# Early modulation of a float32 two-block kernel: nine weight tiles as TensorE's stationary operand, seven on VectorE

## The reference, cut to what matters

```python
def adaln(cond, w, b):
    m = jax.nn.silu(cond) @ w + b
    return jnp.split(m, 3, axis=-1)           # shift, scale, gate

h  = rms_norm(x,   norm_g[0]) * (1 + scale)   + shift      # c     -> shift, scale
hc = rms_norm(ctx, norm_g[0]) * (1 + scale_c) + shift_c    # c_ctx -> shift_c, scale_c
p, pc = h @ w_in, hc @ w_in[:, COL_K:]        # attention and state-space mixer follow
```

## Time and profile before

| | us |
|---|---|
| median of 3 runs (2713.63 to 2717.82) | 2715.2 |
| the profiled execution's own time | 2714.01 |
| its span | 2711.8 |
| TensorE busy, of the span | 2670.9 (98%) |
| VectorE busy | 1667.5 (61%) |
| ScalarE busy | 467.1 (17%) |
| start of the first projection on TensorE, from the span's start | 133.39 |

### The profile page before, as it was taken

The page is one execution under the profiler, slowest core; times in us unless marked ns, Lnnn a source line. Parts: engine busy times, 40 slices in busy tenths (PEclk is TensorE's granted clock), DMA queues, the critical chain, the costliest instruction groups (busy, mean ns, idle before and its releaser), DMA issues. The chain is left out here.

```text
span 2711.8 us, 45920 instructions
## 1 busy us (share of the span) xinstructions
PE 2670.9 (98%) x19376; PEld 2409.5 (89%) x19376; DVE 1667.5 (61%) x2875; ACT 467.1 (17%) x918; POOL 51.3 (2%) x72
## 2 busy tenths in 40 slices
PE   6999999999999999999999999999999999999999
PEld 1399999999997877777778999999999999999999
DVE  3686767776675566666655536556566655555643
ACT  0231211121111222222220002111111111121211
POOL 0000000000000000000000000000000000000000
PEclk9999999999999999999999999999999999999999
DMA  9855755575545333333354455555554554455542
GB/s 387 306 166 198 228 179 182 187 243 169 187 152 183 115 113 113 112 112 112 112 201 154 149 164 171 171 163 177 156 180 159 155 156 146 144 150 158 162 136 82
DMA packets 381819, 453.86 MB, mean 167 GB/s; under 512 B 20596, under 2 KB 351848, under 8 KB 380648
## 3 DMA queue, kind: packets, MB, share of 16 engines
q1 hardware_dynamic: 351520, 356.69, 42.8%
q0 software_dynamic: 19520, 75.50, 7.7%
q10 hardware_dynamic: 10632, 19.51, 1.9%
HBM read 443.49 MB, written 8.19 MB: 167 GB/s over the span
## 5 line engine op out<-in xcount | busy, mean ns | idle before, releaser
L583 PE MATMUL bank<-hT,w 128*128 128x128 f32 (+2 forms) x6240 | 898.1, 302 | 6.1 <-ACT hT L1295 4.6
L583 PEld LDWEIGHTS bank<-hT,w 128*128 128x128 f32 x6240 | 786.7, 193 | 100.0 <-issue 85.4
L583 PE MATMUL bank<-yT,w 128*128 128x128 f32 (+1 forms) x3776 | 526.3, 299 | 1.0 <-DVE yT L2228 1.0
L583 PEld LDWEIGHTS bank<-yT,w 128*128 128x128 f32 x3776 | 493.2, 192 | 22.8 <-DVE yT L2228 1.2
L1295 ACT ACTIVATE work<-bank 128x512 f32<-128x512 f32 (+3 forms) x294 | 151.5, 522 | 1264.1 <-PE bank L583 1212.1
L583 PE MATMUL bank<-hT,work 128*128 128x128 f32 x2672 | 316.8, 275 | 0.0
L583 PEld LDWEIGHTS bank<-hT,work 128*128 128x128 f32 x2672 | 307.5, 192 | 0.0
L583 PEld LDWEIGHTS bank<-w,hT 128*128 128x128 f32 x1792 | 245.0, 191 | 19.3 <-issue 5.7
L583 PE MATMUL bank<-w,hT 128*128 128x128 f32 (+2 forms) x1792 | 261.4, 305 | 0.0
L1295 ACT ACTIVATE work<-work 128x512 f32<-128x512 f32 (+3 forms) x299 | 168.3, 569 | 276.1 <-DVE work L2078 156.3
L1923 DVE SCALAR_TENSOR_TENSOR work<-xT,silc,work 128x512 f32<-128x512 f32 x240 | 180.3, 751 | 33.5 <-DMA xT<-in_ada_w 26.7
(11 more groups left out here) (219 smaller groups left out, 2432.4 us busy)
## 6 DMA issues: line engine op xcount, KB each, us to landing
w<-in_na_ssd_w_in SPq DMA_DIRECT2D x48, 2048.0 KB, 11.4
xT<-in_ada_w POOLq DMA_DIRECT2D x64, 1024.0 KB, 8.6
w<-in_sc_w_in SPq DMA_DIRECT2D x32, 2048.0 KB, 10.2
w<-in_w_in SPq DMA_DIRECT2D x32, 2048.0 KB, 9.9
w<-in_na_ssd_w_out SPq DMA_DIRECT2D x16, 2048.0 KB, 9.5
w<-in_ada_w SPq DMA_DIRECT2D x12, 2048.0 KB, 12.0
w<-in_na_ssd_w_in SPq DMA_DIRECT2D x16, 1024.0 KB, 8.7
w<-in_sc_w_out SPq DMA_DIRECT2D x8, 2048.0 KB, 8.3
```

The lines of the kernel that those rows point to most:

```text
L583: return nc.tensor.matmul(dst, lhsT, rhs, start=start, stop=stop, skip_group_check=free)
```

## The change

Only the early part is written anew.

- TensorE takes nine tiles: (b 2, q 3) and all of blocks 0 and 1. The 128x128 pieces of the tile are now the **stationary** operand and the two columns of `sil` move: 32 matmuls a tile, each of two moving columns, that accumulate over the chunks and quarters straight into columns of bank 0 (shift) and bank 3 (scale). The rows in PSUM, VectorE's copies of them and `early_turn` go.
- VectorE takes seven tiles: all of block 3 and q 0 to 2 of block 2, through three places (`w[3]`, the low half of `yT`, and half of `hT` in 1 KB pieces), loaded by POOL's queue. Two `early_sums` of 16 matmuls each add its two accumulators to bank 3.
- The scale is finished first; VectorE does ten of the sixteen chunks of `first_norm(0)` before it takes the shift, which TensorE's last tile completes.
- `x` and `ctx` are turned apart, 32 transposes behind tile 0 and 32 behind tile 1; ScalarE alone copies them out, a bank (128x512) at a time. ScalarE squares the rows of the tokens with a running sum, and four small VectorE operations put the sums on diagonals (`diagonals`), in place of the reduction over 8192 elements a partition.
- `c` and `c_ctx` are loaded first, as 32 rows of their own; the other parameters come later. The last tile and the first projection's weights are loaded in halves. `x_columns` is stored after three loads of projection weights.

Core of the diff (blank lines left out):

```diff
-    arow = L(2, 4 * TILE)
-    eacc = L(2, 4 * TILE)
+    eaccs = {2: L(2, 4 * TILE), 3: L(2, 4 * TILE)}
+    crow, squares_of_rows, one_zero = L(P), L(4), L(4)
...
-    EARLY = 4
+    EARLY_PE = [(2, 3)] + [(b, q) for b in range(2) for q in range(4)]
+    EARLY_DVE = [(3, q) for q in range(4)] + [(2, q) for q in range(3)]
+    EARLY_SLOT = [0, 1, 2, 0, 1, 2, 1, 2, 3]
+    EARLY_PLACE = [0, 1, 2, 0, 1, 2, 1]
+    EARLY = [EARLY_SLOT.count(s) for s in range(SLOTS)]
...
+    early_places = [w3.rearrange("p (a b) -> p a b", a=4),
+                    yT[:, 0:DC, :].rearrange("p a b -> p (a b)").rearrange("p (a b) -> p a b", a=4),
+                    hT[:, :, 0:T]]
...
-        for t in range(4):
-            wait(gp, early_taken, t)
-            gp.dma_start(w3.rearrange("p (a b) -> p a b", a=4), w_ada[0][:, 4 * t:4 * t + 4, 12 * TILE:16 * TILE]).then_inc(
-                early_in, 16)
+        for t, (b, q) in enumerate(EARLY_DVE):
+            place = EARLY_PLACE[t]
+            earlier = [m for m in range(t) if EARLY_PLACE[m] == place]
+            if earlier:
+                gp.wait_ge(early_taken, earlier[-1] + 1)
+            if place < 2:
+                gp.dma_start(early_places[place], early_columns(b, q)).then_inc(early_v[place], 16)
+            else:
+                for kc in range(4):
+                    gp.dma_start(hT[:, 4 * kc:4 * kc + 4, 0:T], early_columns(b, q, (kc,)).rearrange(
+                        "p a (b c) -> p (a b) c", c=T)).then_inc(early_v[place], 16)
...
-        sp.dma_start(cst[:, :], ins["consts"]).then_inc(consts_in, 16)
+        sp.dma_start(IDENT, ins["consts"][:, 0:P]).then_inc(c_in, 16)
+        for k, src in enumerate((ins["c"][0], ins["c_ctx"])):
+            sp.dma_start(crow[16 * k:16 * k + 16, :], src.rearrange("(a b) -> a b", b=P)).then_inc(c_in, 16)
...
-        for u in range(12):
-            wait(sp, ada_used, u - 2)
-            sp.dma_start(early(u % 3), w_ada[0][:, 4 * (u % 4):4 * (u % 4) + 4, (u // 4) * 4 * TILE:(u // 4 + 1) * 4 * TILE]
-                         ).then_inc(w_loaded[u % 3], 16)
-        sp.wait_ge(xt_dve, DC // 2)
-        sp.wait_ge(xt_act, DC // 2)
-        sp.dma_start(x_scratch, xT[:, :, :].rearrange("p a b -> p (a b)")).then_inc(x_saved, 16)
+        for t, (b, q) in enumerate(EARLY_PE[:8]):
+            earlier = [m for m in range(t) if EARLY_SLOT[m] == EARLY_SLOT[t]]
+            if earlier:
+                sp.wait_ge(ada_used, earlier[-1] + 1)
+            sp.dma_start(early(EARLY_SLOT[t]), early_columns(b, q)).then_inc(w_loaded[EARLY_SLOT[t]], 16)
+        sp.wait_ge(early_taken, 4)
+        b, q = EARLY_PE[8]
+        sp.dma_start(early(3)[:, 0:2, :], early_columns(b, q, (0, 1))).then_inc(early_half, 16)
+        sp.dma_start(early(3)[:, 2:4, :], early_columns(b, q, (2, 3))).then_inc(w_loaded[3], 16)
...
+                sp.wait_ge(ada_used, (4, 7, 8)[n])
...
+        def rows_turned(k):
+            pe.wait_ge((x_in, ctx_in)[k], 32)
+            for m in range(EIGHT):
+                n = EIGHT * k + m
+                wait(pe, xt_act, n - 1)
+                for c in range(2):
+                    for tb in range(2):
+                        last = tr(bank[(1, 5)[n % 2]][:, (2 * c + tb) * P:(2 * c + tb + 1) * P],
+                                  xrow[:, 2 * k + tb, (2 * m + c) * P:(2 * m + c + 1) * P])
+                last.then_inc(xt_pe, 1)
...
+        def early_place(b, ch):
+            at = (b % 2) * 16 + ch * 2
+            return bank[0 if b < 2 else 3][:, at:at + 2]
+        def early_tile(t):
+            b, q = EARLY_PE[t]
+            s = EARLY_SLOT[t]
+            if t < 8:
+                pe.wait_ge(w_loaded[s], 16 * (1 + EARLY_SLOT[:t].count(s)))
+            else:
+                pe.wait_ge(early_half, 16)
             tile = w[s][:, :, :].rearrange("p a b -> p (a b)").rearrange("p (a b) -> p a b", a=4)
             for kc in range(4):
-                for half in range(2):
-                    last = mm(rows_of[half][0:2, :], pair[:, 4 * q + kc, :],
-                              tile[:, kc, half * 512:(half + 1) * 512], q + kc == 0, q + kc == 6)
+                if t == 8 and kc == 2:
+                    pe.wait_ge(w_loaded[3], 16)
+                for ch in range(8):
+                    last = mm(early_place(b, ch), tile[:, kc, ch * P:(ch + 1) * P], pair[:, 4 * q + kc, :],
+                              t < 2 and kc + ch == 0, t == 8 and kc + ch == 10, True)
             last.then_inc(ada_used, 1)
-            if u == 5:
-                pe.wait_ge(x_in, 64)
-                for kc in range(DC):
-                    x_turned(kc)
-            if u == 6:
-                early_turn(0)
-                pe.wait_ge(params_in, 16 * 17)
-                for n in range(1, 4):
-                    last = tr(bank[2][:, n * P:(n + 1) * P], prm[:, n, :])
-                last.then_inc(cols_pe, 1)
-            if u == 10:
-                early_turn(1)
+        def early_sums(b):
+            for ch in range(8):
+                for k in range(2):
+                    last = mm(early_place(b, ch), eaccs[b][:, k, ch * P:(ch + 1) * P], one_zero[:, 2 * k:2 * k + 2],
+                              False, b == 2 and ch + k == 8, True)
+            return last
+        early_tile(0)
+        rows_turned(0)
+        early_tile(1)
+        rows_turned(1)
+        early_tile(2)
+        pe.wait_ge(params_in, 16 * 19)
+        for n in range(4):
+            last = tr(bank[2][:, n * P:(n + 1) * P], prm[:, n, :])
+        last.then_inc(cols_pe, 1)
+        early_tile(3)
+        early_tile(4)
+        pe.wait_ge(consts_in, 16)
         pe.wait_ge(cols_dve, 2)
         norm_sums(0, T + TC)
+        early_tile(5)
         pe.wait_ge(early_taken, 4)
-        for ch in range(8):
-            for k in range(2):
-                n = 64 + 4 * ch + 2 * k
-                last = mm(bank[0][:, n:n + 2], eacc[:, k, ch * P:(ch + 1) * P], ONES[:, 0:2])
-        last.then_inc(ada_turned, 1)
-        early_turn(2)
+        early_sums(3)
+        early_tile(6)
+        early_tile(7)
+        pe.wait_ge(early_taken, 7)
+        early_sums(2).then_inc(ada_used, 1)
+        early_tile(8)
...
+            for k, columns in enumerate((xT, cxT)):
+                for m in range(EIGHT):
+                    n = EIGHT * k + m
+                    act.wait_ge(xt_pe, n + 1)
+                    A(columns[:, 2 * m:2 * m + 2, :], bank[(1, 5)[n % 2]][:, :].rearrange("p (a b) -> p a b", a=2),
+                      ACT.Copy).then_inc(xt_act, 1)
+                wait(act, norm_sq, k)
+                for tb in range(2):
+                    last = A(hT[:, EIGHT * tb:EIGHT * (tb + 1), T:2 * T],
+                             xrow[:, 2 * k + tb, :].rearrange("p (a b) -> p a b", a=EIGHT), ACT.Square,
+                             accum_out=squares_of_rows[:, 2 * k + tb:2 * k + tb + 1])
+                last.then_inc(norm_sq, 1)
...
+        def diagonals():
+            dve.wait_ge(c_in, 48)
+            dve.wait_ge(norm_sq, 2)
+            for tb in range(4):
+                last = v.tensor_scalar(ssq[:, tb * P:(tb + 1) * P], IDENT, squares_of_rows[:, tb:tb + 1], None, ALU.mult)
+            last.then_inc(norm_sum, 1)
...
+        for t in range(3):
+            early_part(t)
         dve.wait_ge(cols_pe, 2)
-        v.tensor_copy(colp[:, P:4 * P], bank[2][:, P:4 * P]).then_inc(cols_dve, 1)
-        early_part(2)
-        early_rows(1)
-        norm_sum_squares(0, 2, T + TC)
-        early_part(3)
-        early_rows(2)
+        v.tensor_copy(colp[:, :], bank[2][:, :]).then_inc(cols_dve, 1)
+        diagonals()
+        for t in range(3, 7):
+            early_part(t)
...
+        first_norm(0, range(10))
+        dve.wait_ge(ada_used, 10)
+        v.tensor_tensor(mod[:, 0, 0:16, :], bank[0][:, 0:32].rearrange("p (a b) -> p a b", b=2), bias[:, 0:16, :],
+                        ALU.add).then_inc(mod_ready, 1)
+        first_norm(0, range(10, DC))
+        amplitude(1, 0, 1)
```

More of the change, by code:

```diff
@@ L610, in tokened @@
             return last
[L613 to L622, removed]
+        pe.wait_ge(c_in, 48)
+        tr(bank[2][:, 0:32], crow[0:32, :], 32).then_inc(cols_pe, 1)
+        def rows_turned(k):
[8 more added lines that the diff above has]
+                last.then_inc(xt_pe, 1)
         def norm_sums(n, width):
@@ L737, in na_unit @@
             if n == 0:
-                featured(bank[0][:, 0:T], s, 0, T, lambda kc: kc + 1).then_inc(acc_full, 1)
+                pe.wait_ge(q_half, 16)
+                featured(bank[0][:, 0:T], s, 0, T, lambda kc: kc + 1, range(EIGHT))
+                pe.wait_ge(w_loaded[0], 16 * (EARLY[0] + 1))
+                featured(bank[0][:, 0:T], s, 0, T, lambda kc: kc + 1, range(EIGHT, DC)).then_inc(acc_full, 1)
                 featured(bank[1][:, 0:T], s, 1, T).then_inc(acc_full, 1)
@@ L1307, in _, with params @@
             rows[f"sc{k}"] = ins["sc_conv_w"][0, k]
-        def params(name, into):
+        def params(name):
```

(46 more changed lines are left out.)

74 lines of the change are left out of this document (29 added, 45 removed).

## The result

The changed kernel takes 2753.1 us against 2714.8 us (medians of four runs each), a ratio of 1.0138 with a 95% interval of 1.0126 to 1.0151: 38.3 us slower. The profiled execution took 2755.46 us, 2.3 above the median of its runs, with a span of 2753.6, 41.8 us longer than before.

A forecast was written before the change was run, and what follows sets the result against it. TensorE's own work, not transfers, was taken to bound the early part: 167.3 us of low-clock work, less 8, plus 1.0 put the first projection at 160.3, +26.9 us, hence 2741 us, range 2727 to 2754.

The forecast's parts named there:

- The likeliest case: Early part on TensorE mostly at the low clock: first projection at 160.3, +26.9 us, 2741 us; chance 0.70.
- the start of tile 0: TensorE's first tile begins at 14.0 us (bounds 12.5 and 16.7), with less constant data ahead on SP's queue.
- The clock falls in a gapless two-column stream: TensorE's early part: two-column matmuls lose the full clock about 5 us after they begin, though the engine never idles.
- rival 1: The full clock holds in TensorE's early tiles: projection begins at 108, -25 us, 2689 us; chance 0.17.
- 13.7 us a tile at the low clock, 7.2 at the full one: Price of a TensorE tile of 32 two-column matmuls, 64 records, against 7.03 before; nine tiles make 123.3 us.
- Sums: TensorE's two sums of 16 matmuls each, 64 records: 13.7 us at the low clock.
- 68 transposes: Transposes on TensorE at 0.214 us each at the low clock: 14.6 us (bounds 9.3 and 20).
- the tail: From TensorE's last early matmul to the first projection: 1.0 us (0.7 to 2.4), against 2.43 before.
- I take 4, twice: -8.: Each group of 32 transposes raises TensorE's clock for a while and gives back 4 us (bounds 0 and 7).
- Rival 2: Transposes on TensorE do not raise the clock, so the -8 goes: 2749 us; chance 0.10.
- Rivals 1 and 3: Full clock for all early tiles (2689 us, chance 0.17), or for about 45% of tile work (2714 us, 0.03).
- VectorE and the other queues off the path: VectorE idles some 15 us behind its third tile, ends near 112; it and the load queues cost nothing.

The follow-up runs named there:

- held_in_before: Kernel before with only its twelve TensorE tiles made the stationary operand with two moving columns, rows' copies and turns gone; 2783.6 us, ratio 1.0245.
- fill_every_4: Changed kernel with one discarded 512-column matmul ahead of every 4 two-column matmuls, from tile 1 on and in the sums; 2757.5 us.
- pool_and_tokens_later: Changed kernel with POOL's second and third tile and the rows of x issued only when TensorE's tile 0 has landed; 2742.7 us.
- tokens_second: Changed kernel with the rows of x issued on ScalarE's queue behind the exponential of c and not first; 2752.8 us.
- pool_later: Changed kernel with POOL's second and third tile issued only when TensorE's first tile has landed; 2752.1 us.
- fill_every_8: Changed kernel with one discarded 512-column matmul ahead of every 8 two-column matmuls, from tile 1 on and in the sums; 2803.5 us.

## Why the prediction was right, and where it was off

It named 2741 us with a range of 2727 to 2754, slower with 0.80; the time is 2753.1. The likeliest case came and its mechanism is the one that the runs show, but the time lies only 0.9 us inside the range, and that is luck: the one term that was far off, the start of tile 0, broke its own bound by 8.7 us, and the profiled execution, 2755.5, lies outside.

- **The clock falls in a gapless two-column stream.** Right. Each stretch after the short rises shows 0.50 with the engine busy all the time, also where every weight load has 128 rows, which was what rival 1 rested on. held_in_before shows it with nothing else changed.
- **13.7 us a tile at the low clock, 7.2 at the full one.** Right: 27.30 and 27.45 for two at the low clock; at the full one a tile with its fillers in fill_every_4 takes 14.0, where 7.2 and 7.0 were added up. Sums 6.8 each (13.7 for both), squares 1.8 (1.7), 68 transposes 14.0 (14.6; some of them ran at the full clock), the tail 0.92 (1.0).
- **The start, "Tile 0 begins at 14.0 (bounds 12.5 and 16.7)".** Wrong, and most of the miss: 25.38, +11.4 us. The step took SP's rate of before, 0.173 MB a us, though before only one POOL tile and the tokens were in flight and these were issued behind SP's tile. With x and POOL's first tile issued ahead of it and two more POOL tiles right behind (x at 0.90 now, at 3.62 before), tile 0's 2.1 MB came at 0.09 MB a us. (The rate also counts from 1.3, the issue of SP's first tile, though the constants in it were issued at 0.89; that moves the step by about 0.1 us.) The prediction knew that three loads "slow SP's", and looked for the cost at the later tiles, not at the first, which nothing covers. With tile 0 early, in pool_and_tokens_later, the start is 159.6 where 160.3 was forecast, and the time 2742.7 where 2741 was: the rest of the sum holds.
- **"I take 4, twice: -8."** Too much in this profile, about right in others. TensorE's own work from tile 0 to the tail took 173.6 - 25.38 = 148.2 us where 145.3 was summed; the nine tiles, 122.9 at 13.65 each, took 118.7, so the rises gave back some 4 us in them, inside the bounds of 0 and 14. In tokens_second, pool_and_tokens_later and pool_later the same work took 144.8, 144.0 and 143.2 us, with longer stretches at the full clock. Together with the start, 11.4 + 2.9 - 0.1 is the 14.2 between 160.3 and 174.5. The medians differ by 38.3 us and not by the profiles' 41.1 at the start, since the profiled execution of the change was the slowest of its four, 2.3 above their median, and that of before 0.8 below its own.
- **Rival 2, transposes do not raise the clock.** Did not come: in the change it rose at 44.7, after 5.7 us of transposes alone. The Trainium skill's "TensorE: Matmul & The Clock Gate", section "Part 4: PE-mode transpose", says that the full clock does not engage for them; by the runs it does, and the measurement decides.
- **Rivals 1 and 3, the full clock for all or for 45% of the tile work.** Did not come: the two rises lasted 3.4 us each. The same page of the Trainium skill, section "What's actually happening", has activity release the clock; taken as rival 1 took it, with a busy engine as the activity, the trace disagrees, with 0.50 granted over 27.00 us in which TensorE was busy 27.00 and its weight loads 27.00.
- **VectorE and the other queues off the path.** Right: it idled 18.4 us where 15 was forecast and ended at 117 where 112 was, with 36 us to spare.

## What to carry to other kernels

Here, in float32, making the large operand stationary and moving two columns saved nothing on TensorE's own account (7.2 us against 7.03 a tile), and in a long stretch of it the clock fell to half (13.7 us a tile); keeping the narrow operand stationary and paying for a copy and a turn was 45 to 47 us faster. Read the granted clock beside the busy time before pricing a matmul, since an engine 100% busy was seen at either clock. And when more loads are put in flight at the start, price the first one that an engine waits for: here it came 11 us later than forecast, while TensorE waited for no other load of weights.

## What the runs showed that was not expected

- A kernel that does more can be faster: with one discarded 512-column matmul to four two-column ones the time is 46 us less than with one to eight, 2757.5 against 2803.5, as the clock was 1.00 or 0.50.
- The same mixture runs at either clock for a while: filler and pieces in the ratio of one to eight had 1.00 from 45.0 to 54.8 us in fill_every_8 and 0.50 from 86 to 225.
- A two-column matmul costs the same 0.21 us a record at the low clock whether its weights have two rows or 128 (13.65/64 in every tile).
- POOL's two further tiles and the tokens did not add up in what they cost tile 0: holding back the one gave 0.8 us, issuing x 3 us later 1.8, holding back both 10.7.
